# Recurrent x projections moved into the Strassen stage of a hybrid decoder block

## The reference

```python
z = h @ w_in[l]
lru_x, lru_y, hq, hf, hi, hg, ca, cg, gate_logits = jnp.split(z, split_idx, axis=-1)
xc = causal_dw_conv(xb, conv_w, conv_b)                    # 4 taps on lru_x
gate_x = sigmoid(blockdiag(xc, wx) + bx); gate_a = sigmoid(blockdiag(xc, wa) + ba)
log_a = min(-8 * gate_a * softplus(-lam), -1e-6)
u = xc * gate_x * sqrt(-expm1(2.0 * log_a))
h = associative_scan(exp(log_a), u);  y_lru = h * gelu(yb)
```

## Time and profile before

| | us |
|---|---|
| median of three runs | 2405.55 (2405.52, 2405.55, 2405.8) |
| span of the profiled execution, first to last instruction | 2404.5 |
| median above that span | 1.05 |
| Strassen stage, from 66 us to | 371.25 |
| recurrence stage, to the first matmul of hf | 589.67 |
| head 0, to about | 652 |

### The profile page before, as it was taken

The page is one execution under the profiler, slowest core; times in us unless marked ns, Lnnn a source line. Parts: engine busy times, 40 slices in busy tenths (PEclk is TensorE's granted clock), DMA queues, the critical chain, the costliest instruction groups (busy, mean ns, idle before and its releaser), DMA issues.

```text
span 2404.5 us, 31465 instructions
## 1 busy us (share of the span) xinstructions
PE 2388.6 (99%) x11815; PEld 1967.3 (82%) x11815; DVE 1676.1 (70%) x1837; ACT 811.7 (34%) x1187; POOL 1253.3 (52%) x936
## 2 busy tenths in 40 slices
PE   9999999999999999999999999999999999999998
PEld 6888888888888888888888888888887888888887
DVE  7889888888878888878865637652896534444464
ACT  4443442554222222221122214253444434342422
POOL 0677773343022332223767766745667656666564
PEclk9999999999999999999999999999999999999999
DMA  7322323111211111124854445522532212121243
GB/s 284 140 80 105 127 110 123 62 61 61 78 44 44 44 44 44 44 97 144 277 199 149 140 140 167 181 91 71 177 129 75 92 62 97 59 99 57 84 175 123
DMA packets 93193, 263.28 MB, mean 109 GB/s; under 512 B 8736, under 2 KB 14112, under 8 KB 92064
## 3 DMA queue, kind: packets, MB, share of 16 engines
q1 hardware_dynamic: 77536, 227.26, 27.3%
q10 hardware_dynamic: 15552, 34.61, 4.1%
HBM read 214.65 MB, written 47.19 MB: 109 GB/s over the span
## 4 chain that ended last, share of the span: by engine, by line
PE 94%; DVE 3%; issue 1%; ACT 1%; DMA 0%; SPq 0%; POOL 0%; ACTq 0%; DVEq 0%
PE ps L537 25%; PE ps L538 25%; PE ps L539 25%; PE xb L537 2%; PE xb L538 2%; PE xb L539 2%; PE xa L537 2%; PE xa L539 2%; PE xa L538 2%; PE ps L630 1%; PE xb L771 1%; PE xb L800 1%; PE xb L803 1%; PE xa L791 1%; DVE mt_lo L1138 0%
## 5 line engine op out<-in xcount | busy, mean ns | idle before, releaser
L2822 POOL TENSOR_TENSOR small<-small 128x1 f32<-128x1 f32 x172 | 53.6, 311 | 794.8 <-PE ps L539 620.9
L2825 POOL TENSOR_TENSOR w_lo<-w_raw,w_hi 128x1024 fp32r<-128x1024 f32 x172 | 444.5, 2584 | 14.4
L537 PE MATMUL ps<-h_hi,w_hi 128*128 128x512 f32 x928 | 368.0, 397 | 0.0
L539 PE MATMUL ps<-h_hi,w_lo 128*128 128x512 f32 x928 | 362.0, 390 | 0.0
L538 PE MATMUL ps<-h_lo,w_hi 128*128 128x512 f32 x928 | 361.7, 390 | 0.0
L2911 POOL TENSOR_TENSOR m_lo<-m_raw,m_hi 128x512 fp32r<-128x512 f32 x144 | 200.3, 1405 | 146.1 <-ACT m_hi L2203 142.8
L537 PE MATMUL ps<-yb_hi,w_hi 128*128 128x512 f32 x608 | 238.7, 393 | 0.0
L539 PE MATMUL ps<-yb_hi,w_lo 128*128 128x512 f32 x608 | 236.6, 389 | 0.0
L538 PE MATMUL ps<-yb_lo,w_hi 128*128 128x512 f32 x608 | 236.6, 389 | 0.0
L537 PEld LDWEIGHTS ps<-h_hi,w_hi 128*128 128x128 f32 x928 | 174.3, 188 | 36.9 <-issue 0.2
L539 PEld LDWEIGHTS ps<-h_hi,w_lo 128*128 128x128 f32 x928 | 174.2, 188 | 37.0
(11 more groups left out here) (432 smaller groups left out, 5587.7 us busy)
## 6 DMA issues: line engine op xcount, KB each, us to landing
w_raw<-wall SPq DMA_DIRECT2D x230, 512.0 KB, 3.4
m_raw<-wall SPq DMA_DIRECT2D x96, 256.0 KB, 2.7
gst<-gate_d SPq DMA_DIRECT2D x24, 512.0 KB, 5.0
x_d<-xx ACTq DMA_DIRECT2D x16, 512.0 KB, 3.6
raw_odd<-wall SPq DMA_DIRECT2D x14, 512.0 KB, 4.2
x_sb<-xT SPq DMA_DIRECT2D x4, 1024.0 KB, 13.2
kv_d<-kv SPq DMA_DIRECT2D x4, 1024.0 KB, 6.6
glu_d<-gbuf SPq DMA_DIRECT2D x8, 512.0 KB, 2.6
```

The lines of the kernel that those rows point to most:

```text
L537: nc.tensor.matmul(out, wh, xh, start=start, stop=False, skip_group_check=onto)
L539: return nc.tensor.matmul(out, wl, xh, start=False, stop=stop, skip_group_check=onto)
L2822: nc.gpsimd.tensor_tensor(small[:, 13:14], small[:, 12:13], small[:, 12:13], ALU.add)
L2825: nc.gpsimd.tensor_tensor(w_lo[:, u], w_raw[:, u], w_hi[:, u].bitcast(F32), ALU.subtract).then_inc(w_split, 1)
```

## The change

Four of the eight pairs of the recurrence stage, the x tiles, become four more steps of the Strassen stage, right after the convolution branch's pairs. `SEVENS` goes from 15 to 19. ScalarE copies these results (`ACT.Copy` in place of the sigmoid) into `sigb` and `gbuf`, SyncE stores them to a new tensor in DRAM (`lru_x_d`) and loads them again for each block of the recurrence (`load_lru`). The ring of six is turned by two slots from product 63 on, so that it ends in the same slots as before; four products there wait for a slot whose last user is four products back instead of six. The sixth convolution block moves into the four added steps (`CONVS` 6), and none is left beside the recurrence.

In the recurrence stage TensorE now makes the two y tiles and then the gate products. ScalarE makes the first tap (scale and bias) and the high part of the gate weights; VectorE makes the other three taps. The chain of block b + 1 (taps, high and low parts) is put between the gated products and the scans of block b on both engines, and the scans of block b come behind the low parts of block b + 1. ScalarE's sigmoid into `lgx` waits for the previous block's product with the gelu row, the gelu rows lie in four buffers of their own, and the second gelu stands ahead of tanh. All loops of the stage but TensorE's are unrolled.

For head 0, VectorE clips hf and makes the low part of hi's weights ahead of the last scan of the last block, and SyncE issues the loads of hf and hq ahead of the store of block 2.

The core of the diff; left out are the changed counts of semaphores, the convolution's row choices, and the order of the weights in DRAM:

```diff
 EARLY = 8
-SEVENS = KB - 1 + EARLY
+LRU_PAIRS = KB // 2
+STORED = LRU_PAIRS + EARLY
+SEVENS = KB - 1 + STORED
 LATE = 3 * KB // 2 - EARLY
-CONVS = 5
+CONVS = 6
...
-N_LRU = N_EARLY + 2 * EARLY
-N_HG = N_LRU + 2 * KB
+N_LRU = N_EARLY + 2 * STORED
+N_HG = N_LRU + KB
...
 RING, FIRST = (0, 4, 5, 1, 2, 3), 6
+TURN = 7 * (KB + 1)
 
 
 def slot_of(n):
 
-    return FIRST if n == 0 else RING[n % len(RING)]
+    return FIRST if n == 0 else RING[(n + (2 if n >= TURN else 0)) % len(RING)]
+
+
+def slot_user(n):
+
+    return max((i for i in range(n) if slot_of(i) == slot_of(n)), default=0)
...
-        lxc_hi = at("lxc_hi", L + 2 * ROW, [P, 2, T], F32R)
-        lxc_lo = at("lxc_lo", L + 4 * ROW, [P, 2, T], F32R)
+        lxc_hi = at("lxc_hi", CONV + 2 * UB + ROW, [P, 2, T], F32R)
+        lxc_lo = at("lxc_lo", CONV + 2 * UB + 3 * ROW, [P, 2, T], F32R)
...
+        lyg = [at(f"lyg{i}", a, [P, T]) for i, a in enumerate((CONV + 128, CONV + UB + 128, CONV + 2 * UB, CONV + 2 * UB + 6 * ROW))]
...
-                        half_of(0, 0)
-                        pe.wait_ge(evac[1], m)
-                        half_of(0, 1).then_inc(mm_done, 1)
-                        continue
-                    full_tile(m + q // 2, q % 2)
+                m = N_LRU // 2 + b
+                if first(b):
+                    pe.wait_ge(w_split, 2 * (m - M0) + 1)
+                    pe.wait_ge(evac[0], m)
+                    pe.wait_ge(evac[1], m - 1)
+                    half_of(0, 0)
+                    pe.wait_ge(evac[1], m)
+                    half_of(0, 1).then_inc(mm_done, 1)
+                else:
+                    full_tile(m, 0)
+                full_tile(m, 1)
                 if first(b):
                     pe.wait_ge(conv_done, CONVS)
-                take(m + 1, 1)
-                half_of(1, 0)
                 pe.wait_ge(lg_split, b + 1)
                 pe.wait_ge(lru_split, 2 * b + 2)
                 for p in range(2):
@@ -736,7 +745,6 @@
                                 mm = mm3(acc[:, cols], lg_hi[:, g, k, w], lg_lo[:, g, k, w],
                                          lxc_hi[:, k, cols], lxc_lo[:, k, cols], k == 0, k == 1)
                         mm.then_inc(lmm_done, 1)
-                half_of(1, 1).then_inc(mm_done, 1)
...
+                    if j < LW - 1:
+                        done(ins)
+                ins.then_inc(xc_ready, 1)
+
+            def lru_low(b, p):
+
+                dve.wait_ge(xc_hi_done, 5 * b + p + 4)
+                if b == 0:
+                    dve.wait_ge(conv_stored, 16 * CONVS)
+                    dve.wait_ge(gate_stored[1], 16 * STORED)
+                low(lxc_lo[:, p], lxc[:, p], lxc_hi[:, p]).then_inc(lru_split, 1)
+
+            def lru_gated(b, p):
+
+                dve.wait_ge(lgate_done, 4 * b + 2 * p + 2)
+                ca = der[:, 2, bass.ds(2 * b + p, 1)]
+                v.tensor_scalar(lga[:, p], lga[:, p], ca, -1e-6, ALU.mult, ALU.min).then_inc(la_ready, 1)
+                mul(lgx[:, p], lgx[:, p], lxc[:, p]).then_inc(la_ready, 1)
+
+            def lru_mult(b, p):
+
+                dve.wait_ge(ldec_done, 2 * b + p + 1)
+                v.scalar_tensor_tensor(ltanh[:, p], lsq[:, p], 1.0, ltanh[:, p], ALU.add, ALU.mult).then_inc(lm_ready, 1)
+
+            def lru_scan(b, p):
+
+                dve.wait_ge(lmult_done, 2 * b + p + 1)
+                dve.wait_ge(la_ready, 4 * b + 2 * p + 4)
+                done(mul(lgx[:, p], lgx[:, p], lsq[:, p]))
+                done(v.tensor_tensor_scan(lga[:, p], ldec[:, p], lgx[:, p], 0.0, ALU.mult, ALU.add))
+                dve.wait_ge(evac[p], N_LRU // 2 + b + 1)
+                if b:
+                    dve.wait_ge(ylru_stored, 16 * b)
+                mul(lgel[:, p], lga[:, p], lyg[2 * (b % 2) + p][:]).then_inc(ylru_ready, 1)
+
+            def clipped_gate(m):
+
+                dve.wait_ge(mm_done, 2 * m + 1)
+                for n in range(2):
+                    ins = v.tensor_scalar(hg["zc"][:, n * HALF:(n + 1) * HALF], turned(ps[0], n), CLIP, -CLIP, ALU.min, ALU.max)
+                ins.then_inc(evac[0], 1)
+
+            def head_weights_low(i, u):
+
+                dve.wait_ge(w_high, 2 * i + u + 2)
+                low(w_lo[:, u], w_raw[:, u], w_hi[:, u]).then_inc(w_split, 1)
+
+            for p in range(2):
+                lru_conv(0, p)
             gate_weights(0)
+            for p in range(2):
+                lru_low(0, p)
             for b in range(KB // 2):
-                m = N_LRU // 2 + 2 * b
+                more = b + 1 < KB // 2
                 for p in range(2):
-                    c = 2 * b + p
-                    dve.wait_ge(evac[p], m + 1)
-                    done(affine(lxc[:, p], lxb[p][:, 0:T], pc(c, LRU_W), pc(c, LRU_B)))
-                    for j in range(1, LW):
-                        ins = v.scalar_tensor_tensor(lxc[:, p], lxb[p][:, j:j + T], pc(c, LRU_W + j), lxc[:, p], ALU.mult, ALU.add)
-                        if j < LW - 1:
-                            done(ins)
-                    ins.then_inc(xc_ready, 1)
-                for p in range(2):
-                    dve.wait_ge(xc_hi_done, 2 * b + p + 1)
-                    low(lxc_lo[:, p], lxc[:, p], lxc_hi[:, p]).then_inc(lru_split, 1)
-
-                conv_units(8 if b < 3 else 9)
-
-                gated = []
-                for p in range(2):
-                    dve.wait_ge(lgate_done, 4 * b + 2 * p + 2)
-                    ca = der[:, 2, bass.ds(2 * b + p, 1)]
-                    v.tensor_scalar(lga[:, p], lga[:, p], ca, -1e-6, ALU.mult, ALU.min).then_inc(la_ready, 1)
-                    gated.append(s.at(mul(lgx[:, p], lgx[:, p], lxc[:, p])))
-                if b + 1 < KB // 2:
+                    lru_gated(b, p)
+                    if more:
+                        lru_conv(b + 1, p)
+                lru_mult(b, 0)
+                if more:
                     gate_weights(b + 1)
-
-                for p in range(2):
-                    dve.wait_ge(ldec_done, 2 * b + p + 1)
-                    v.scalar_tensor_tensor(ltanh[:, p], lsq[:, p], 1.0, ltanh[:, p], ALU.add, ALU.mult).then_inc(lm_ready, 1)
-                for p in range(2):
-                    dve.wait_ge(lmult_done, 2 * b + p + 1)
-                    s.wait(gated[p])
-                    done(mul(lgx[:, p], lgx[:, p], lsq[:, p]))
-                    s.wait(s.at(v.tensor_tensor_scan(lga[:, p], ldec[:, p], lgx[:, p], 0.0, ALU.mult, ALU.add)))
-                    dve.wait_ge(evac[p], m + 2)
-                    mul(lgel[:, p], lga[:, p], lgel[:, p]).then_inc(ylru_ready, 1)
+                lru_mult(b, 1)
+                if more:
+                    for p in range(2):
+                        lru_low(b + 1, p)
+                lru_scan(b, 0)
+                if not more:
+                    clipped_gate(N_HG // 2)
+                    head_weights_low(HEAD_PAIR, 0)
+                lru_scan(b, 1)
 
 
             def left(x, c):
...
@@ -2262,7 +2295,7 @@
                     u, odd = {0: (0, 0), 5: (0, 1), 6: (1, 1)}[i]
                     act.wait_ge(s_loaded[s_ % 2][u], 16 * (s_ // 2 + 1))
                     if n >= len(RING):
-                        act.wait_ge(seven_done, n + 1 - len(RING))
+                        act.wait_ge(seven_done, slot_user(n) + 1)
                     elif n:
                         act.wait_ge(mm_done, N_CONF + (1 if slot < 2 else 2))
                     full = raw_half(s_, u, odd)
...
-            def sigmoid_part(out_, n, x):
-
-                return a.activation(out_[:, n * HALF:(n + 1) * HALF], x, ACT.Sigmoid)
+            def sigmoid_part(s_, out_, n, x):
+
+                of_lru = KB - 1 <= s_ < KB - 1 + LRU_PAIRS
+                return a.activation(out_[:, n * HALF:(n + 1) * HALF], x, ACT.Copy if of_lru else ACT.Sigmoid)
 
             block_high(0)
             for n in range(3):
...
-
-            def gelu(m, p):
-
-                act.wait_ge(mm_done, 2 * m + p + 3)
-                a.activation(lgel[:, p], ps[p][:], ACT.Gelu_apprx_tanh).then_inc(evac[p], 1)
...
+            sigmoid_part(SEVENS - 1, gbuf, 0, x_bank(SEVENS - 1)).then_inc(evac[1], 1)
+
+
+            def gelu(b, p):
+
+                act.wait_ge(mm_done, 2 * (N_LRU // 2 + b) + p + 1)
+                if b == 1 and p == 0:
+                    act.wait_ge(gate_stored[0], 16 * STORED)
+                if b > 1:
+                    act.wait_ge(ylru_ready, 2 * b + p - 3)
+                a.activation(lyg[2 * (b % 2) + p][:], ps[p][:], ACT.Gelu_apprx_tanh).then_inc(evac[p], 1)
+
+            def lru_first_tap(b, p):
+
+                act.wait_ge(lx_loaded[p], 16 * (b + 1))
+                act.wait_ge(la_ready, 4 * b + 2 * p if b else p + 1)
+                a.activation(lxc[:, p], lxb[p][:, 0:T], ACT.Identity, bias=pc(2 * b + p, LRU_B), scale=pc(2 * b + p, LRU_W)).then_inc(xc_hi_done, 1)
+
+            def lru_weights_high(b):
+
+                act.wait_ge(lg_loaded, 16 * b + 16)
```

(85 more changed lines are left out.)

87 lines of the change are left out of this document (39 added, 48 removed).

## The result

The changed kernel takes 2411.89 us (median of 11 runs, 2410.2 to 2414.03) against 2405.77 for the kernel before (11 runs, 2405.4 to 2406.77): slower by 6.1 us, ratio 1.0026 with a 95% interval of 1.0017 to 1.0034. The forecast was no change, 2404.9, range 2397.0 to 2409.5.

A forecast was written before the change was run, and what follows sets the result against it. TensorE, busy 2388.6 of 2404.5 us, was taken as the bound; -11.7 removed work, +8.0 recurrence waits and +3.1 head 0 gave -0.6, a span of 2403.9, plus 1.05 for the median: 2404.9 us, range 2397.0 to 2409.5.

The forecast's parts named there:

- the 1.05 that was taken for the median above the span: Whole kernel: the runs' median stands 1.05 us above the profiled span, taking 2403.9 to 2404.9.
- Added steps: Strassen stage: four added steps take 76.16 us, 19.04 each, with TensorE waiting nowhere new.
- the turned ring: Strassen stage: four slots lose two products of lead, 5.4 us; cost taken as 0.
- rival (3): Recurrence stage and head 0: tanh after a gelu needs one more table load per block, 1.28 us; 2408.5, chance 0.07.
- Failed step 1: Strassen and recurrence stages: added steps plus remaining recurrence work take 206.72 against 218.42, 11.7 us less.
- The collision: Recurrence scans: a GpSimd split adds 3.0 us; TensorE waits 3.4 in blocks 2 and 3, 1.2 before block 2's gates.
- Rival (2): Recurrence chain: a second GpSimd split meets gated products or low parts, 3.0 us more in three blocks; 2413.9, chance 0.08.
- Failed step 2: Gate products' second half: the sigmoid (1.12) follows the scan at 7.7, ends at 8.8; TensorE wants its bank at 5.4.
- Failed step 3: Recurrence stage and head 0: TensorE's waits entered at their own length, 8.0 and 3.1 us, with no clock term.
- Failed step 4: Behind head 0, including the up projection: no term in the sum, a change of 0.
- Head 0: Head 0: TensorE waits 2.2 us for the queries and another 0.9, together 3.1; ends 0.9 and 4.4.
- The 0.9 for the first level: Head 0, after the diagonal blocks and a quarter tile: TensorE waits another 0.9 us for VectorE's diagonal part.

The follow-up runs named there:

- run 5: The changed kernel with the low parts of eight y, hf and hq weight tiles made by VectorE instead of GpSimd: 2402.58 us.
- run 8: The changed kernel with only the second tile's low part of each pair made by VectorE, GpSimd keeping the first tile's: 2404.49 us.
- run 9: The changed kernel with only the first tile's low part made by VectorE, ahead of the scans, GpSimd keeping the second tile's: 2413.65 us.
- Run 1: The changed kernel with a one-column sigmoid on ScalarE behind the first gelu of blocks 1 to 3, ahead of the first sigmoid's waits: 2407.53 us.
- run 3: The changed kernel with ScalarE's high part of the up projection's fourth weight tile put ahead of the issue of a store: 2408.79 us.
- run 4: The kernel before with a 128-column copy on ScalarE ahead of the high part of the MLP's fourth weight tile: 2408.16 us.
- run 2: The changed kernel with the scan's product written into ltanh and the scan into lsq, sigmoids waiting for the product alone: 2407.13 us.
- run 6: The kernel of run 5 with the early high part of the MLP's fourth weight tile as well: 2401.27 us.

## Why the prediction was wrong

The measured 2411.89 lies 7.0 above the forecast and above its range. On the span the sum was short by 5.8: 2.8 of removed work, 1.4 of clock in block 2, 0.8 in head 0 and 3.3 in the up projection, less 2.1 of waits in the gate products that did not come and 0.4 of all the rest. Another 0.9 is the 1.05 that was taken for the median above the span, and the median lies 0.3 above the profiled execution.

**Added steps: right.** The Strassen stage grew by 383.93 - 307.80 = 76.13 (76.16), with TensorE busy throughout, so the turned ring cost nothing, as taken, and x for block 0 cost 0.2. The first tap on ScalarE took 1.25 (1.2). Five table loads a block and none for tanh: rival (3) did not occur.

**Failed step 1: "together 206.72 against 218.42: 11.7 us less".** It came as 8.9. The sum priced the gate products at the pace of the tiles, 10.9 a block; they take 11.28, and with the waits' 0.5 that are shown too short this is 1.9 of the missing 2.8.

**The collision: right as a mechanism, wrong in its places.** Runs 5, 8 and 9 show that the low part in the scans of half 0 is the price. It was put at 3.4 in each of blocks 2 and 3 and 1.2 ahead of block 2's gates, 8.0 in all; it came as 0.85, 4.2 and 0.85 in the second halves of blocks 1 to 3, 5.9 in all. That the two sums lie so near is in part luck: blocks 1 and 3 wait for a table load that the sum did not have, and block 3 was spared the collision in half 0. Rival (2) came true at one place, the tanh product ahead of block 2. The Trainium skill, SBUF — State Buffer, section SBUF: two separate sides, has VectorE and GpSimd share a pair of ports as an exclusive lock; the rows of block 2 agree with it, where the product ends 1.07 behind the low part that it met.

**Failed step 2: "the sigmoid may only then write `lgx`, so 8.8".** The term lacked the table load that follows the gelu. In the earlier trace rows a load starts as soon as the activation ahead of it ends; here the sigmoid has two waits, and the load stands behind the second. Run 1 prices it at 0.85 to 1.4 in each block. The Trainium skill, ScalarE: Activation LUTs, section Step-by-step: what each stage is for, says that the load is placed right before its activation; the trace agrees and shows that the wait can lie ahead of both.

**Failed step 3: a wait costs its own length.** Behind three of the waits, 4.2, 2.2 and 1.9 us long, seven matmuls ran at 1.2 GHz: 4.2 us that no term held. Net it is about 3.4, since at full clock head 0 would be only 0.8 shorter (below) and the up projection 1.2 (46.52 instead of 47.69).

**Failed step 4: nothing changes behind head 0.** The forecast ended there. Runs 3 and 4 show that 0.3 us on ScalarE 1100 us later decide between 0 and 2.2 (3.3 with the clock). Why ScalarE came late there in the changed kernel stays open.

**Head 0: right.** The wait for the queries was put at 2.2 and is 2.2. The 0.9 for the first level do not show as a wait here, because the clock fell ahead of it. Runs 3 and 5, whose clock stays up, wait 0.6 there, and from the first score block to the first matmul behind the second they take 5.87 instead of 6.68.

## What to carry to other kernels

Where TensorE is always busy, an edit that saves its work is paid for by the engine that must now hurry. Count for that engine every instruction of another engine that it cannot run beside, not its own work alone: here eight low parts, at 1.2 us each on VectorE, took 9.3 us off the kernel once GpSimd no longer made them. Give each wait of TensorE a second price, for the slower matmuls that may follow it (0.8 to 1.4 us here), and look where the table of an activation is loaded, before its wait or behind it. And compare the whole of two traces, by stages, to the last instruction: 3.3 of the 5.2 us lay far from the change.

## What the runs showed of the hardware that was not expected

Between its first and its last matmuls TensorE's clock fell only in waits or within 1.6 us of their end. It fell each time at the four of 2.8 to 5.4 us in block 2 (the changed kernel, runs 1, 3 and 9; 7 to 10 matmuls at 0.43). At waits of 2.2 to 2.8 us in head 0 it fell in the changed kernel and in runs 1, 2, 6, 8 and 9, and not in runs 3 and 5; at one of 2.2 before block 3's gate products it did not fall (run 2). At those of about 1.9 in the up projection it fell in the changed kernel and not in runs 2, 4, 5, 8 and 9. What decides between these is open.

Which of VectorE and GpSimd gets through first hangs on tenths of a microsecond, and not on the two starts alone. A low part that started 0.19 ahead of VectorE's step went through at once (kernel before, 1778.15). One that started 0.14 behind the start of a step got in behind that step, and VectorE's next step waited and took 2.87 (run 1, 1774.30). In the changed kernel one that started 0.09 behind the start of a step (1780.34) let the sum behind that step pass as well. What decides between the last two is open.

GpSimd's high part, which reads one row and writes one, holds VectorE up too: in run 5, where GpSimd makes only the high parts of these tiles, the product with the gelu row beside one (536.41, 1.97 long) takes 1.89 instead of 1.2.
